# A feed-forward step with three of four k-tile groups by seven products, its down sums by ScalarE copy and accumulating DMA

## The chip, the cores and the metric

The kernel runs on one core of one Trainium2 chip. The metric is the time of one execution on the device in microseconds (us), as the median of three runs. Five engines of the core matter: TensorE (PE in the rows) multiplies, VectorE (DVE) and ScalarE (ACT) work elementwise on SBUF and PSUM, GpSimd (POOL) and SyncE (SP) issue DMAs here. Each works through its own list in order; semaphores tie the lists together.

## What is computed

One decoder layer for 256 tokens of width 2048 in float32: a feed-forward block, a mixing block with two attentions, a second feed-forward block, and a final norm. The change touches the two feed-forward blocks alone:

```python
def swiglu(x, w_gate, w_up, w_down):
    return (jax.nn.silu(x @ w_gate) * (x @ w_up)) @ w_down

x = x + 0.5 * swiglu(rmsnorm(x, ffn1_norm[l]), ffn1_w_gate[l], ffn1_w_up[l], ffn1_w_down[l])
...
x = x + 0.5 * swiglu(rmsnorm(x, ffn2_norm[l]), ffn2_w_gate[l], ffn2_w_up[l], ffn2_w_down[l])
```

The gate and up matrices are 2048 x 5632, the down matrix is 5632 x 2048.

## The kernel before

**Numbers in two parts.** Every float32 weight and activation is split into a rounded part (`hi`, made by ScalarE) and the rest (`lo`, made by VectorE), and each product of two matrices takes three matmuls: hi x hi, hi x lo, lo x hi.

**Slabs.** Weights arrive by DMA in pieces of 1 MB into `raw`, which has 4 places (`LOADS`). The unit of all three engines is a slab of 128 x 1024 weights. ScalarE rounds slab n into a ring of 6 places (`FFN_RING`; `w_hi` and `more_hi`) as soon as TensorE has finished slab n-6; VectorE then subtracts to get the `lo` half (`w_lo`, `more_lo`); TensorE multiplies. An ordinary slab is 12 matmuls of 512 columns (two k-tiles, two token tiles, three parts); a slab of kind "paired" holds one of the products below and is 6 matmuls.

**Chunks and steps.** The 5632 hidden columns are 11 chunks of 512. The first chunk's gate and up come in 16 slabs (`FIRST`). Then follow 10 steps (`STEPS`) of 30 slabs (`STEP`). Step i computes gate and up of chunk i+1 and multiplies chunk i's hidden values by the down matrix (the last 8 slabs, `DOWN`). The last chunk's down is in `last_down`. Nine steps are a loop with one step in its body; the tenth is written out.

**Seven products.** The 16 k-tiles are 4 groups of 4. For a group, two token tiles by (gate, up) is a 2 x 2 matrix product over pairs of k-tiles. In groups 1 and 3 ("paired") it is done by seven products (`PRODUCTS`) rather than eight, with sums of weights `T1` to `T4` (made by VectorE into `sums`) and sums of activations `S1` to `S4` (made once per block: `sum_pairs`, `split_pairs`). Groups 0 and 2 ("direct") are multiplied as they are, in 4 ordinary slabs. The seven results end in PSUM banks, and VectorE adds them up (lines 1397 to 1415 of the kernel before; semaphore `combined`).

**Around them.** When the products are added up, ScalarE applies silu and VectorE multiplies (`multiply_up`) into `hidden`. In the next step TensorE transposes it, the two token tiles one after the other through the same PSUM bank (`T`; `transpose_tokens`), ScalarE rounds (`round_tokens`) and VectorE splits each into `hT_hi` and `hT_lo` (`split_tokens`, line 1291). The second transpose waits until VectorE has read the first from the bank (`ht_lo`). Each of the four 512-column pieces of the down result is scaled by 0.5 and added to `xres` by VectorE from PSUM (`add_down`, line 1311).

The order is written out by hand: each engine's `step` goes over o = 0 to 29; ScalarE and VectorE at place o first handle slab o+6. SyncE loads a piece when `lo_ready` shows that the last user of its place is through (`FREE`).

Of the kernel before, what the change touches and what calls it, by code (L numbers as in the profile page):

```python
# [54 lines left out]
FIRST, STEP = 2 * WIDE, 30  # L55
# [19 lines left out]
PAIRED = {0: 0, 11: 1}  # L75
DIRECT = {7: 0, 18: 2}
T3, T1, T2, T4 = 0, 1, 2, 3
S1, S2, S3, S4 = 0, 1, 2, 3
PAIR_SLABS = 7

PRODUCTS = (("sum", T3), ("up", 1), ("sum", T1), ("sum", T2), ("sum", T4), ("gate", 1), ("gate", 0))
SUMS = 8 * STEPS

FREE = (-6, -4, -2, 0, 2, 7, 9, 11, 13, 18, 20, 22)
GROUP_ORDER = (1, 0, 3, 2)


def step_slab(r):

    for first, g in PAIRED.items():  # L90
        if first <= r < first + PAIR_SLABS:
            return "paired", g, r - first
    for first, g in DIRECT.items():
        if first <= r < first + 4:
            return "direct", g, r - first
    return "down", None, r - (STEP - DOWN)
# [27 lines left out]
class Place:  # L124
# [3 lines left out]
    def __init__(self, start, load, per=0, loads=0, i=None):  # L128
# [8 lines left out]
        assert per % self.ring == 0  # L137
# [5 lines left out]
    def slot(self, offset):  # L143
        return (self.start + offset - self.origin) % self.ring
# [15 lines left out]
def step_place(f, i=None):  # L160
    return Place(FFN_START[f] + FIRST, FFN_LOAD[f] + FIRST_LOADS, STEP, STEP_LOADS, i)


def final_step_place(f):
    return Place(FFN_START[f] + FIRST + (STEPS - 1) * STEP, FFN_LOAD[f] + FIRST_LOADS + (STEPS - 1) * STEP_LOADS)
# [6 lines left out]
def build(nc, x, ffn1_norm, ffn1_w_gate, ffn1_w_up, ffn1_w_down, mix_norm, w_in, b_forget,  # L172
# [39 lines left out]
    sums = nc.alloc_sbuf_tensor_at("sums", [P, 4, 2, CH], F32, offset=qT_at)  # L212
    pair_hi = nc.alloc_sbuf_tensor_at("pair_hi", [P, 4, 4, P], F32R, offset=kT_at)
    pair_lo = nc.alloc_sbuf_tensor_at("pair_lo", [P, 4, 4, P], F32R, offset=kT_at + 16 * P * 4)
# [72 lines left out]
    def step_source(r):  # L287

        kind, g, o = step_slab(r)
        if kind == "down":  # L290
            l = STEP_LOADS - NN + o // 2
            return raw[:, l % LOADS, o % 2 * 2:o % 2 * 2 + 2, :], l
        if kind == "direct":
            l = 2 * GROUP_ORDER.index(g) + o // 2
            return raw[:, l % LOADS, o % 2 * 2:o % 2 * 2 + 2, :], l
        what, which = PRODUCTS[o]
        if what == "sum":
            return sums[:, which], None
        l = 4 * g + (what == "gate")
        return raw[:, l % LOADS, which::2, :], l  # L300
# [23 lines left out]
    combined = sem("combined")  # L324
    hi_ready = sem("hi_ready")
# [55 lines left out]
    ADDED = {0: 2, "mix": 2 + FF_CHUNKS * NN, 1: 2 + (FF_CHUNKS + NN) * NN}  # L381
    ADDED_ALL = ADDED[1] + FF_CHUNKS * NN
# [13 lines left out]
    with block:  # L396

        @block.sync
        def _(sp):
# [27 lines left out]
            def ffn(f):  # L427
# [12 lines left out]
                with sp.Fori(0, STEPS) as i:  # L440
                    place = step_place(f, i)
                    cols = bass.ds(i * CH + CH, CH)
                    for l, g in enumerate(GROUP_ORDER):
                        order = (up_w, gate_w) if g % 2 else (gate_w, up_w)
                        for half, w in enumerate(order):
                            load_step(place, 2 * l + half, w[f][:, CT * g:CT * (g + 1), cols])
                    for n in range(NN):
                        load_step(place, 2 * NN + n, down_w[f][:, bass.ds(i * CT, CT), n * CH:(n + 1) * CH])
# [68 lines left out]
        def _(pe):  # L517
# [112 lines left out]
            def paired(place, offset, g):  # L630

                def of_pair(s):
                    return lambda j: (pair_hi[:, s, 2 * g + j], pair_lo[:, s, 2 * g + j])

                def of_tile(odd, t):
                    return lambda j: of_x(CT * (2 * g + 1) + 2 * j + odd, t)

                for o, (bank, lhs) in enumerate((
                        (M7, of_pair(S3)), (UP0, of_pair(S4)), (M5, of_pair(S1)), (M6, of_pair(S2)),
                        (GATE + 1, of_tile(1, 1)), (GATE, of_tile(1, 0)), (M1, of_tile(0, 0)))):  # L640
                    yield o
                    whole = bank in (M7, M5, M1, M6)
                    product(place, offset + o, bank, lhs, g == 0, whole and g == 1)

            def ffn(f, b):

                def step(place, i, last):
                    hid, base, merged = i * TT + HID[f], i * NN + ADDED[f], (i + f * STEPS) * COMBINED
                    for o in paired(place, 0, 0):
                        if o == 1:  # L650

                            pe.wait_ge(added, base - 1)
                        if o == 2:
                            transpose_tokens(hid, 0, T)
                        if o == 4:

                            pe.wait_ge(hidden_ready, hid + TT)
                            pe.wait_ge(added, base)

                    pe.wait_ge(ht_lo, hid + 1)  # L660
                    transpose_tokens(hid, 1, T)
                    for g, first in ((0, 7), (2, 18)):
                        if g == 2:
                            for o in paired(place, 11, 1):
                                pass
                        for o in range(2):
# [945 lines left out]
```

## Time and profile before

| | us |
|---|---|
| median of 3 runs (lowest, highest) | 2107.26 (2106.88, 2107.4) |
| the profiled execution: time, span of its rows | 2106.82, 2105.0 |
| TensorE busy | 2081.9 |
| VectorE busy | 1611.0 |
| ScalarE busy | 1095.1 |

The span runs from the first to the last recorded instruction; 1.8 us of the profiled execution lie around it. "Busy" counts instructions at work; a matmul's row is longer than its share of the engine, because matmuls overlap, so the distance between starts is what one costs.

### The profile page before, as it was taken

Reading aid. Unit: us, or ns where it says so; the run is one execution under the profiler, and the core shown is the slowest. Engines: PE = TensorE matmul, PEld = TensorE weight load, DVE = VectorE, ACT = ScalarE, POOL = GpSimd, SP = SyncE. Lnnn points to the kernel's source line nnn. Section 1 sums busy time; section 2 is a strip of 40 time slices with the busy share of each in tenths; the row PEclk is TensorE's granted clock in tenths of the full one; section 3 lists DMA queues with packets and bytes.
Section 4 is the critical chain, followed back from the end, with each engine's and each line's share of the span. In section 5 each row is a group of like instructions: output and inputs, shape, how many; then the busy total and the mean of one; then the engine's idle time right before and its main releaser. Section 6 shows DMA issues by size and latency. Waiting matters only on the chain.

```text
span 2105.0 us, 26528 instructions
## 1 busy us (share of the span) xinstructions
PE 2081.9 (99%) x9475; PEld 1727.4 (82%) x9475; DVE 1611.0 (77%) x1613; ACT 1095.1 (52%) x1259; POOL 2.6 (0%) x7
## 2 busy tenths in 40 slices
PE   8999999999999999999999999999999999999997
PEld 6888888888888888888888888888888888888886
DVE  7988988899888744444455655688998888998886
ACT  6555555554555444554554344465555555555553
POOL 0000000000000000000000000000000000000000
PEclk9999999999999999999999999999999999999999
DMA  7655556555565455545445655556565655465652
GB/s 270 220 189 189 199 199 212 204 177 204 190 209 200 140 182 196 181 160 170 159 154 197 200 198 192 188 185 215 170 212 185 219 203 203 163 219 179 219 204 96
DMA packets 202452, 402.88 MB, mean 191 GB/s; under 512 B 6417, under 2 KB 6593, under 8 KB 202273
## 3 DMA queue, kind: packets, MB, share of 16 engines
q1 hardware_dynamic: 202032, 401.64, 56.2%
q8 instruction: 34, 0.56, 0.1%
q0 software_dynamic: 160, 0.46, 0.1%
q14 instruction: 18, 0.14, 0.0%
q10 hardware_dynamic: 208, 0.08, 0.0%
HBM read 400.06 MB, written 2.10 MB: 191 GB/s over the span
## 4 chain that ended last, share of the span: by engine, by line
PE 95%; DVE 2%; ACT 1%; DMA 1%; issue 1%; SPq 0%; ACTq 0%; DVEq 0%
PE ps L530 21%; PE ps L532 21%; PE ps L531 21%; PE ps L545 6%; PE ps L543 6%; PE ps L544 6%; PE ps L707 3%; PE ps L709 3%; PE ps L708 3%; PE ps L595 1%; DMA raw<-in_ffn_w_gate 1%; DVE w_lo L1201 0%; PE ps L718 0%; PE ps L779 0%; ACT w_hi L922 0%
## 5 line engine op out<-in xcount | busy, mean ns | idle before, releaser
L1201 DVE TENSOR_TENSOR w_lo<-raw,w_hi 128x1024 fp32r<-128x1024 f32 x256 | 312.8, 1224 | 303.4 <-ACT w_hi L922 303.2
L922 ACT ACTIVATE w_hi<-raw 128x1024 fp32r<-128x1024 f32 x256 | 270.2, 1059 | 310.7 <-PE ps L532 310.5
L935 ACT ACTIVATE w_hi<-raw 128x1024 fp32r<-128x1024 f32 x280 | 297.0, 1061 | 221.9 <-PE ps L709 98.7
L1235 DVE TENSOR_TENSOR w_lo<-raw,w_hi 128x1024 fp32r<-128x1024 f32 x280 | 342.1, 1222 | 79.5 <-ACT w_hi L935 66.2
L530 PE MATMUL ps<-w_hi,xT_hi 128*128 128x512 f32 x816 | 321.3, 394 | 2.7 <-DVE w_lo L1201 2.7
L532 PE MATMUL ps<-w_hi,xT_lo 128*128 128x512 f32 x816 | 318.6, 390 | 0.0
L531 PE MATMUL ps<-w_lo,xT_hi 128*128 128x512 f32 x816 | 318.2, 390 | 0.0
L1235 DVE TENSOR_TENSOR more_lo<-raw,more_hi 128x1024 fp32r<-128x1024 f32 x160 | 195.6, 1223 | 43.5 <-ACT more_hi L935 34.1
L935 ACT ACTIVATE more_hi<-raw 128x1024 fp32r<-128x1024 f32 x160 | 169.6, 1061 | 110.7 <-PE ps L532 87.1
L530 PE MATMUL ps<-w_hi,hT_hi 128*128 128x512 f32 x576 | 224.4, 390 | 0.0
L532 PE MATMUL ps<-w_hi,hT_lo 128*128 128x512 f32 x576 | 224.1, 389 | 0.0
L531 PE MATMUL ps<-w_lo,hT_hi 128*128 128x512 f32 x576 | 224.1, 389 | 0.0
L935 ACT ACTIVATE w_hi<-sums 128x1024 fp32r<-128x1024 f32 x120 | 127.7, 1064 | 181.1 <-PE ps L532 94.4
L530 PEld LDWEIGHTS ps<-w_hi,xT_hi 128*128 128x128 f32 x816 | 153.7, 188 | 33.6 <-issue 3.1
L532 PEld LDWEIGHTS ps<-w_hi,xT_lo 128*128 128x128 f32 x816 | 153.5, 188 | 32.4
L531 PEld LDWEIGHTS ps<-w_lo,xT_hi 128*128 128x128 f32 x816 | 153.7, 188 | 30.8
L1235 DVE TENSOR_TENSOR w_lo<-sums,w_hi 128x1024 fp32r<-128x1024 f32 x120 | 146.5, 1221 | 7.7 <-ACT w_hi L935 4.6
L1311 DVE SCALAR_TENSOR_TENSOR xres<-ps,xres 128x1024 f32<-128x1024 f32 x104 | 126.8, 1219 | 14.1 <-PE ps L532 14.1
L532 PEld LDWEIGHTS ps<-w_hi,hT_lo 128*128 128x128 f32 x576 | 108.1, 188 | 22.5
L531 PEld LDWEIGHTS ps<-w_lo,hT_hi 128*128 128x128 f32 x576 | 108.1, 188 | 22.4
L530 PEld LDWEIGHTS ps<-w_hi,hT_hi 128*128 128x128 f32 x576 | 108.1, 188 | 22.3
L709 PE MATMUL ps<-w_hi,xT_lo 128*128 128x512 f32 x320 | 124.5, 389 | 0.0
(218 smaller groups left out, 3583.6 us busy)
## 6 DMA issues: line engine op xcount, KB each, us to landing
raw<-in_ffn_w_gate SPq DMA_DIRECT2D x88, 1024.0 KB, 5.0
raw<-in_ffn_w_up SPq DMA_DIRECT2D x88, 1024.0 KB, 5.0
raw<-in_ffn_w_down SPq DMA_DIRECT2D x88, 1024.0 KB, 5.1
raw<-in_w_in SPq DMA_DIRECT2D x80, 1024.0 KB, 5.0
raw<-in_w_out SPq DMA_DIRECT2D x16, 1024.0 KB, 5.0
raw<-in_w_proj_dil SPq DMA_DIRECT2D x8, 1024.0 KB, 5.1
raw<-in_w_proj_fox SPq DMA_DIRECT2D x8, 1024.0 KB, 5.0
xres<-in_x SPq DMA_DIRECT2D x4, 512.0 KB, 7.1
```

The source lines that it names most:

```text
L530: nc.tensor.matmul(acc, hi, hi_w[:, j], start=first and j == 0, stop=False)
L531: nc.tensor.matmul(acc, hi, lo_w[:, j], start=False, stop=False)
L532: done = nc.tensor.matmul(acc, lo, hi_w[:, j], start=False, stop=last and j == 1)
L543: nc.tensor.matmul(acc, hi, hi_w[:, j], start=first and j == 0, stop=False)
L544: nc.tensor.matmul(acc, hi, lo_w[:, j], start=False, stop=False)
L545: done = nc.tensor.matmul(acc, lo, hi_w[:, j], start=False, stop=last and j == 1)
L709: done = nc.tensor.matmul(acc, lo, hi_w[:, j], start=False, stop=last and j == 1)
L922: nc.scalar.activation(slot_hi(place, offset), raw_half(place, offset), ACT.Copy).then_inc(hi_ready, 1)
L935: nc.scalar.activation(slot_hi(place, offset), src, ACT.Copy).then_inc(hi_ready, 1)
L1201: nc.vector.tensor_tensor(slot_lo(place, offset), raw_half(place, offset), slot_hi(place, offset).bitcast(F32), ALU.subtract).then_inc(lo_ ...
L1235: nc.vector.tensor_tensor(slot_lo(place, offset), step_source(r)[0], slot_hi(place, offset).bitcast(F32), ALU.subtract).then_inc(lo_ready, 1)
L1311: nc.vector.scalar_tensor_tensor(xres[:, :, chunk(n)], ps[:, banks:banks + TT], factor, xres[:, :, chunk(n)], ALU.mult, ALU.add)\
```

## The change

- Groups 1, 2 and 3 go by seven products, group 0 is direct. A step has 33 slabs: products 0 to 6 and 7 to 13 (two groups in a row), 4 direct slabs (14 to 17), products 18 to 24, down slabs 25 to 32. The order within the seven is new.
- The four weight sums share two places of `sums` (`SUM_PLACE`): `T3` and `T2` one, `T1` and `T4` the other; `T4` is made one slab later than before.
- In all steps but the last of each block the down result goes another way: ScalarE copies each pair of banks, scaled by 0.5, into one of two halves of `gate_buf` (semaphore `down_copied`), and GpSimd issues a DMA that adds it to `xres` (`accum_op`; semaphores `down_added`). ScalarE's third and fourth copy first wait for the first and second DMA to land.
- The transposes of the hidden tiles stand before slabs 5 and 9 (before: 2 and 7), ScalarE's and VectorE's parts of them at places 6 and 10 (before: 2 and 5). The adding up moves to places 22 to 28.
- 33 is no multiple of the ring of 6, so a loop body of TensorE, ScalarE and VectorE holds two steps.

The core of the diff:

```diff
-FIRST, STEP = 2 * WIDE, 30
+FIRST, STEP = 2 * WIDE, 33
...
-PAIRED = {0: 0, 11: 1}
-DIRECT = {7: 0, 18: 2}
+PAIR_AT, PAIR_GROUPS, PAIR_SLABS = (0, 7, 18), (1, 2, 3), 7
+DIRECT_AT, DIRECT_GROUP = 14, 0
-PRODUCTS = (("sum", T3), ("up", 1), ("sum", T1), ("sum", T2), ("sum", T4), ("gate", 1), ("gate", 0))
+PRODUCTS = (("sum", T3), ("gate", 0), ("sum", T1), ("sum", T2), ("up", 1), ("sum", T4), ("gate", 1))
+SUM_PLACE = {T3: 0, T2: 0, T1: 1, T4: 1}
-FREE = (-6, -4, -2, 0, 2, 7, 9, 11, 13, 18, 20, 22)
+FREE = (-6, -4, -2, 0, 5, 7, 12, 14, 16, 18, 23, 25)
...   TensorE, step
-                    for o in paired(place, 0, 0):
+                    for o in paired(place, 0):
...
-                        if o == 2:
-                            transpose_tokens(hid, 0, T)
+                        if o == 5:
+                            transpose_tokens(hid, 0, T)
...
+                    for o in paired(place, 1):
+                        if o == 2:
+                            pe.wait_ge(ht_lo, hid + 1)
+                            transpose_tokens(hid, 1, T)
-                        pe.wait_ge(combined, merged + (1, 3, 5, 4)[n])
+                        pe.wait_ge(combined, merged + (1, 3, 4, 5)[n])
...   ScalarE, step
+                        if not last and o > DOWN_AT and (o - DOWN_AT) % 2 == 1:
+                            n = (o - DOWN_AT) // 2
+                            earlier = f * (STEPS - 1) + (n >= 2)
+                            act.wait_ge(slab_done, place.slab(o + 1))
+                            if not (type(i) is int and i + earlier == 0):
+                                act.wait_ge(down_added[(n + 2) % NN], i * 16 + earlier * 16)
+                            nc.scalar.activation(gate_buf[:, n % 2], ps[:, banks:banks + TT], ACT.Copy,
+                                                 scale=0.5).then_inc(down_copied, 1)
...   GpSimd
+            for j in range(2 * (STEPS - 1)):
+                for n in range(NN):
+                    pool.wait_ge(down_copied, j * NN + n + 3)
+                    if j > 0:
+                        pool.wait_ge(down_added[n], j * 16)
+                    pool.dma_start(xres[:, :, n * CH:(n + 1) * CH], gate_buf[:, n % 2],
+                                   accum_op=ALU.add).then_inc(down_added[n], 16)
...   VectorE, weight_sum and step
+                if kind == "paired" and o in (1, 2, 4):
+                    weight_sum(place, q, pair, {1: T1, 2: T2, 4: T4}[o], count)
+                if r + 1 in PAIR_AT:
+                    weight_sum(place, q, PAIR_AT.index(r + 1), T3, count)
-                        if o > STEP - DOWN and o % 2 == 1:
+                        if last and o > DOWN_AT and (o - DOWN_AT) % 2 == 1:
...
-                        if o == 2:
+                        if o == 6:
                             split_tokens(hid, 0, T)
-                        if o == 5:
+                        if o == 10:
                             split_tokens(hid, 1, T)
-                        if o == 18:
+                        if o == 22:
...
-                with dve.Fori(0, STEPS - 1) as i:
-                    step(step_place(f, i), i, False)
+                with dve.Fori(0, STEPS // 2 - 1) as i:
+                    for s in range(2):
+                        step(step_place(f, s, 2, i), i * 2 + s, False)
```

**VectorE at the start of a step.** The rows are those of the step written out last, where no loop's register rows stand between. `sums<-` rows are weight sums, `w_lo` and `more_lo` rows are splits of slabs, `hT_lo` rows the splits of the two token tiles. Before, from the split of slab 6 to that of the second token tile:

```order
L1235 TENSOR_TENSOR more_lo<-raw,more_hi 128x1024 [waits hi_ready] x2
L1235 TENSOR_TENSOR w_lo<-raw,w_hi 128x1024 [waits hi_ready]
L1291 TENSOR_TENSOR hT_lo<-ps,hT_hi 128x4x128 [waits ht_hi]
L1235 TENSOR_TENSOR w_lo<-raw,w_hi 128x1024 [waits hi_ready]
L1208 TENSOR_TENSOR sums<-raw 128x1024 [waits raw_landed0]
L1235 TENSOR_TENSOR w_lo<-raw,w_hi 128x1024 [waits hi_ready]
L1235 TENSOR_TENSOR w_lo<-sums,w_hi 128x1024 [waits hi_ready]
L1291 TENSOR_TENSOR hT_lo<-ps,hT_hi 128x4x128 [waits ht_hi]
```

Now, from the weight sum ahead of slab 6 (the first `hT_lo` row is the first token tile; slabs 6 to 12 stand before it):

```order
L1250 TENSOR_TENSOR sums<-raw 128x1024 [waits raw_landed2,lo_ready]
L1276 TENSOR_TENSOR w_lo<-raw,w_hi 128x1024 [waits hi_ready]
L1276 TENSOR_TENSOR w_lo<-sums,w_hi 128x1024 [waits hi_ready]
L1254 TENSOR_TENSOR sums<-raw 128x1024 [waits raw_landed3,lo_ready]
L1276 TENSOR_TENSOR w_lo<-raw,w_hi 128x1024 [waits hi_ready]
L1258 TENSOR_TENSOR sums<-sums,raw 128x1024 [waits summed,lo_ready]
L1276 TENSOR_TENSOR more_lo<-sums,more_hi 128x1024 [waits hi_ready] x2
L1262 TENSOR_TENSOR sums<-raw,sums 128x1024 [waits summed,lo_ready]
L1276 TENSOR_TENSOR w_lo<-raw,w_hi 128x1024 [waits hi_ready]
L1276 TENSOR_TENSOR w_lo<-sums,w_hi 128x1024 [waits hi_ready]
L1332 TENSOR_TENSOR hT_lo<-ps,hT_hi 128x4x128 [waits ht_hi]
```

Before, three splits (slabs 6 to 8) stood ahead of the first token tile; now there are seven (slabs 6 to 12) and four weight sums.

**TensorE at the second transpose.** Again the last written-out step. Before, the last three matmuls of slab 6, the second transpose, which waits for `ht_lo`, and the start of slab 7, a direct one:

```order
L543 MATMUL ps<-more_hi,xT_hi 128x512
L544 MATMUL ps<-more_lo,xT_hi 128x512
L545 MATMUL ps<-more_hi,xT_lo 128x512
L595 MATMUL ps<-tab,hidden 128x128 [waits hidden_ready,ht_lo]
L595 MATMUL ps<-tab,hidden 128x128 x3
L530 MATMUL ps<-more_hi,xT_hi 128x512 [waits lo_ready]
L531 MATMUL ps<-more_lo,xT_hi 128x512
L532 MATMUL ps<-more_hi,xT_lo 128x512
```

Now, the last three of slab 8, the transpose, and the start of slab 9, a product:

```order
L552 MATMUL ps<-w_hi,xT_hi 128x512
L553 MATMUL ps<-w_lo,xT_hi 128x512
L554 MATMUL ps<-w_hi,xT_lo 128x512
L604 MATMUL ps<-tab,hidden 128x128 [waits hidden_ready,ht_lo]
L604 MATMUL ps<-tab,hidden 128x128 x3
L552 MATMUL ps<-w_hi,pair_hi 128x512 [waits lo_ready]
L553 MATMUL ps<-w_lo,pair_hi 128x512
L554 MATMUL ps<-w_hi,pair_lo 128x512
```

The second transpose stands nine products into the step, where it stood seven in; between the two transposes there are four products (slabs 5 to 8), where there were five (slabs 2 to 6).

**ScalarE in the down part.** Before, only roundings of slabs and the two rows of silu stood there. Now, from the first copy to the fourth, in the ninth step of a block (`gate_buf` rows are the copies, the other `raw` and `sums` rows the roundings):

```order
L1074 ACTIVATE gate_buf<-ps 128x1024 [waits down_added2,slab_done]
L950 ACTIVATE w_hi<-sums 128x1024 [waits slab_done,summed]
L998 ACTIVATE chunk_buf<-chunk_buf,rstd 128x512 [waits rstd_ready,combined]
L998 ACTIVATE chunk_buf<-chunk_buf,rstd 128x512
L950 ACTIVATE w_hi<-raw 128x1024 [waits slab_done,raw_landed1]
L1074 ACTIVATE gate_buf<-ps 128x1024 [waits down_added3,slab_done]
L950 ACTIVATE w_hi<-sums 128x1024 [waits slab_done,summed]
L950 ACTIVATE more_hi<-sums 128x1024 [waits slab_done,summed]
L1074 ACTIVATE gate_buf<-ps 128x1024 [waits down_added0,slab_done]
L950 ACTIVATE more_hi<-raw 128x1024 [waits slab_done,raw_landed0]
L950 ACTIVATE w_hi<-sums 128x1024 [waits slab_done,summed]
L1074 ACTIVATE gate_buf<-ps 128x1024 [waits down_added1,slab_done]
```

The four copies are new; roundings of slabs stand between them, and each waits for the DMA that last read its half of `gate_buf`.

## Rows read from the trace of the kernel before

**Rows 1.** The page, busy us (share of the span) xinstructions, and the chain's shares

```profile
PE 2081.9 (99%) x9475; PEld 1727.4 (82%) x9475; DVE 1611.0 (77%) x1613; ACT 1095.1 (52%) x1259; POOL 2.6 (0%) x7
...
PE 95%; DVE 2%; ACT 1%; DMA 1%; issue 1%; SPq 0%; ACTq 0%; DVEq 0%
```

**Rows 2.** Waits of TensorE: engine line waited for, us, times, longest

```profile
PE ps L576 <- DMA xres<-in_x: 6.1, 1, 6.1
PE ps L530 <- DVE w_lo L1201: 2.7, 1, 2.7
```

**Rows 3.** Line 1400 (once a step), 300 to 420 us: durations ns, first and last start

```profile
L1400 DVE TENSOR_TENSOR partial<-ps,partial x2: 691/691/691, 351.3 to 414.8; 128x512 f32<-128x512 f32 x2
```

**Rows 4.** Window of one step: stretch, length, busy of TensorE, its loads, VectorE, ScalarE

```profile
314.60:378.10 63.50, 63.50 (x286) 52.56 (x285) 56.65 (x51) 34.32 (x35) 0.00 (x0) 1.00 0.57 198
```

**Rows 5.** Timeline of TensorE, end of a step and start of the next

```profile
303.67 0.39 PE L530 MATMUL ps<-w_hi,hT_hi 128*128 128x512 f32 x1
...
313.87 0.39 PE L530 MATMUL ps<-w_hi,hT_hi 128*128 128x512 f32 x1
...
314.55 0.39 PE L543 MATMUL ps<-more_hi,pair_hi 128*128 128x512 f32 x1
...
317.27 0.60 PE L595 MATMUL ps<-tab,hidden 128*128 128x128 f32 x4
317.63 0.48 PE L543 MATMUL ps<-w_hi,pair_hi 128*128 128x512 f32 x1
...
320.46 0.39 PE L543 MATMUL ps<-w_hi,xT_hi 128*128 128x512 f32 x1
```

**Rows 6.** Timeline of VectorE around the same place and later in the step

```profile
301.35 1.41 DVE L1305 SCALAR_TENSOR_TENSOR hidden<-up_sums,rstd,chunk_buf 128x512 f32<-128x512 f32 x2
...
305.01 1.22 DVE L1224 TENSOR_TENSOR sums<-raw 128x1024 f32<-128x1024 f32 x1
...
311.81 2.54 DVE L1235 TENSOR_TENSOR w_lo<-sums,w_hi 128x1024 fp32r<-128x1024 f32 x2
...
315.89 1.22 DVE L1235 TENSOR_TENSOR w_lo<-raw,w_hi 128x1024 fp32r<-128x1024 f32 x1
...
321.54 0.68 DVE L1291 TENSOR_TENSOR hT_lo<-ps,hT_hi 128x512 fp32r<-128x512 f32 x1
...
349.45 1.23 DVE L1235 TENSOR_TENSOR more_lo<-raw,more_hi 128x1024 fp32r<-128x1024 f32 x1 [1.49 <-ACT more_hi L935]
350.59 0.68 DVE L1397 TENSOR_TENSOR partial<-ps,partial 128x512 f32<-128x512 f32 x1
```

**Rows 7.** Timeline of ScalarE, the same step

```profile
314.75 1.06 ACT L935 ACTIVATE w_hi<-raw 128x1024 fp32r<-128x1024 f32 x1 [1.66 <-PE ps L532]
...
346.60 0.58 ACT L1049 ACTIVATE partial<-ps 128x512 f32<-128x512 f32 x1
```

**Rows 8.** DMA issues of the whole run: KB each, median us to landing

```profile
tab<-shape_tables POOLq DMA_DIRECT2D x1, 384.0 KB, 6.3
...
f_raw<-in_w_in POOLq DMA_DIRECT2D x1, 64.0 KB, 7.4
```

**Rows 9.** Windows at launch: stretch, length, PE busy, granted clock, DMA share, GB/s

```profile
10.00:14.00 4.00, 1.30 (x5) 0.93 1.05 387
14.00:16.00 2.00, 2.00 (x7) 0.50 1.05 387
16.00:18.00 2.00, 2.00 (x9) 0.79 1.06 388
```

**Rows 10.** Timeline of TensorE at launch

```profile
13.81 0.63 PE L530 MATMUL ps<-w_hi,xT_hi 128*128 128x512 f32 x1
...
16.80 0.42 PE L531 MATMUL ps<-w_lo,xT_hi 128*128 128x512 f32 x1
```

**Rows 11.** Timelines at launch, of GpSimd and then of VectorE

```profile
16.03 0.68 POOL L1185 DMA_DIRECT2D tab<-shape_tables  x1 [15.58 <-ACT xT_hi L947]
...
16.70 2.36 DVE L1201 TENSOR_TENSOR w_lo<-raw,w_hi 128x1024 fp32r<-128x1024 f32 x2 [0.25 <-ACT w_hi L922]
```

More of the change, by code:

```diff
@@ L287, in step_source @@
     def step_source(r):
[L289 to L300, printed above, removed]
+        kind, pair, o = step_slab(r)
+        if kind == "paired":
+            what, which = PRODUCTS[o]
+            if what == "sum":
+                return sums[:, SUM_PLACE[which]], None
+            l = PAIR_LOADS[pair][what == "gate"]
+            return raw[:, l % LOADS, which::2, :], l
+        l = DIRECT_LOADS[o // 2] if kind == "direct" else DOWN_LOADS + o // 2
+        return raw[:, l % LOADS, o % 2 * 2:o % 2 * 2 + 2, :], l
     ident = tab[:, C_ID:C_ID + P]
@@ L324, in build @@
     combined = sem("combined")
+    down_copied = sem("down_copied")
+    down_added = [sem(f"down_added{n}") for n in range(NN)]
     hi_ready = sem("hi_ready")
@@ L674, in step @@
+                    for o in range(2):
+                        slab(place, DIRECT_AT + o, (GATE, GATE + 1), of_x, CT * DIRECT_GROUP + 2 * o,
+                             False, False)
+                    pe.wait_ge(ht_lo, hid + TT)
+                    for o in range(2):
+                        direct_up(place, DIRECT_AT + 2 + o, CT * DIRECT_GROUP + 2 * o, o == 0, o == 1)
+                    for o in paired(place, 2):
+                        pass
                     for n in range(NN):
-                        pe.wait_ge(combined, merged + (1, 3, 5, 4)[n])
+                        pe.wait_ge(combined, merged + (1, 3, 4, 5)[n])
@@ L706, in direct_up @@
                         begin = first and j == 0 and t == 1
+                        end = last and j == 1 and t == 1
                         nc.tensor.matmul(acc, hi, hi_w[:, j], start=begin, stop=False)
                         nc.tensor.matmul(acc, hi, lo_w[:, j], start=False, stop=False)
-                        done = nc.tensor.matmul(acc, lo, hi_w[:, j], start=False, stop=last and j == 1)
+                        done = nc.tensor.matmul(acc, lo, hi_w[:, j], start=False, stop=end)
                 done.then_inc(slab_done, 1)
@@ new lines, in step @@
+                        if last and o == DOWN_AT + 4:
+                            for n in (2, 3):
+                                act.wait_ge(down_added[n], (f + 1) * (STEPS - 1) * 16)
+                            round_hidden(i * TT + HID[f] + TT, last_hi, A)
+                for s in range(2):
+                    step(step_place(f, s), s, False)
+                with act.Fori(1, STEPS // 2 - 1) as i:
+                    for s in range(2):
+                        step(step_place(f, s, 2, i), i * 2 + s, False)
@@ L1234, in split_step @@
+                kind, pair, o = step_slab(r)
+                if kind == "paired" and o in (1, 2, 4):
+                    weight_sum(place, q, pair, {1: T1, 2: T2, 4: T4}[o], count)
+                if r + 1 in PAIR_AT:
+                    weight_sum(place, q, PAIR_AT.index(r + 1), T3, count)
+                if r == STEP - 1 and not final:
+                    weight_sum(place, q + 1, 0, T3, count)
                 dve.wait_ge(hi_ready, place.slab(offset + 1))
```

256 lines of the change are left out of this document (126 added, 130 removed).

## Prediction

> **What bounds the kernel now.** I read the page first: TensorE is busy for 2081.9 of 2105.0 us, and the chain that ended last runs through it for 95% [rows 1]. Its list of waits says how close to its limit it is: after the first microseconds of launch (6.1 and 2.7 us) nothing over 1.0 us is in it [rows 2]. So a matmul less is time gained, and a new wait of TensorE is time lost; everything else counts only through these two.
>
> The sizes come from the timelines. Matmuls start 0.2267 us apart: from 303.67 to 313.87 us there are 45 steps, 10.20 / 45 [rows 5]. A product slab (6 matmuls) is 1.36 us, an ordinary one (12) 2.72. A transpose of one token tile takes 317.27 to 317.63, and the two products behind it 2.83 (to 320.46) instead of 2.72, so it costs 0.36 + 0.11 = 0.47 [rows 5]. A step of before is 276 matmuls and two transposes, 62.57 + 0.94 = 63.51 us; line 1400, which runs once a step, comes back after 414.8 - 351.3 = 63.5 [rows 3]. The sum closes, so no wait hides in a step, and TensorE is busy throughout [rows 4].
>
> VectorE's operations of 1024 columns start 1.133 us apart when it has work: six of them lie between 305.01 and 311.81 [rows 6]. Their results are ready 1.22 after the start.
>
> **The change, part by part.**
>
> *Matmuls.* 30 slabs with 14 products were 14 x 6 + 16 x 12 = 276 matmuls; 33 slabs with 21 products are 21 x 6 + 12 x 12 = 270. Six fewer are 1.36 us a step, 27.2 us in 20 steps. This part is nearly certain.
>
> *VectorE's load.* A step gains 3 splits and 4 weight sums and loses 4 additions of the down result: 3 x 1.133 = 3.4 us more, in steps that are to be shorter. In a step of before it was busy for 56.65 of 63.50 us [rows 4], so the sum over a step still fits. What counts is where the work stands.
>
> *The stretch of 14 products.* I take time 0 at the first product of a step; in the trace it is 314.55 [rows 5]. ScalarE can round slab 5 once the last down slab is through: it started 0.20 after time 0 (314.75) and took 1.06 [rows 7], so with 0.04 for the hand-over VectorE starts on slab 5 at 1.30. (In the trace it did so at 315.89, 1.34, with an addition ahead of it [rows 6].) This holds it at the start of every step, however early it was before. Up to the split of the first token tile its list now has 12 operations: slabs 5 to 12 and the sums T3, T1, T2, T4 of the second group. 12 x 1.133 = 13.60. Three times a sum and the split of its slab have one other operation between them, while sum, hand-over, rounding and hand-over take 1.22 + 0.04 + 1.06 + 0.04 = 2.36 against 2 x 1.133; that adds 0.09 each, 0.27. The token split starts at 15.17 and takes 0.68 [rows 6]; at 15.9 TensorE may go on. TensorE reaches the second transpose after nine products and one transpose, 9 x 1.36 + 0.47 = 12.71. It waits **3.2 us, in every step**. Before, the same split was done at 321.54 + 0.68, which is 7.67 after time 0, and wanted at 7 x 1.36 + 0.47 = 9.99: it had 2.3 us to spare. What is queued behind the waiting transpose is all of TensorE's work. After it VectorE has slack again (four direct slabs of 2.72 us), so nothing is late next. Bounds: without the 0.27 and with the quickest hand-overs 2.9; with 2% on VectorE's operations 3.5.
>
> *The start of the down part.* Its first bank pair waits for the first addition behind slab 28's split, which needs slab 22 done. From the end of slab 22: 0.20, rounding 1.06, 0.04, then split to addition 1.14 (349.45 to 350.59), addition 0.68 [rows 6, 7], 0.05: 3.17. TensorE has two products for it, 2.72. A wait of 0.45, between 0.3 and 0.6. Before, it had two direct slabs and more.
>
> *The tenth step.* Here the hidden tiles are wanted within the step, after the fourth down slab. That is at 21 x 1.36 + 8 x 2.72 + 0.94 + 3.2 + 0.45 = 54.9. VectorE starts the first partial addition at 54.9 - 10.88 - 0.05 - 0.68 = 43.3; it and the second take 1.3 together, then seven operations at 1.133 (slabs 29 to 32, two additions of the up result, one of the down result) lead to the adding up of the gate, at 52.5; then slab 33; a down addition that must wait for slab 28 (54.9 and 0.2, so 55.1); slab 34 at 56.2; the multiplication at 57.4. Its first half is ready 0.7 later (1.41 for both [rows 6]). TensorE waits 3.3, and 0.2 for the second tile: 3.5 us, twice in the program, 7.0. Bounds 5 and 9.
>
> *Down sums.* ScalarE takes on four copies a step. 512 columns from PSUM took 0.58 [rows 7], so 1024 take at most 1.16; ScalarE is busy for half the span [rows 1]. At the start of a step the fourth copy makes slab 6's rounding late by 0.7 us, but VectorE comes to slab 6 later still (3.57, behind T3). The third copy waits for the DMA issued after the first. From copy to copy there are four down slabs, 10.9 us; less the copy of 1.1, the transfer has 9.8 us from GpSimd's start. The trace has no accumulating DMA. The nearest rows are GpSimd's two: 6.3 us for 384 KB, and 7.4 for 64 KB in 2048 short pieces [rows 8], both beside full queues (share 1.05 in [rows 9]). Scaled by bytes, 6.3 x 512 / 384 = 8.4, an estimate that leaves 1.4. I cost it at nothing; the lower bound is nothing too, the upper one is 12 us, if reading the destination adds as much as half the transfer: 2.2 us late, in 18 steps, 40 us. GpSimd's issue did not slow VectorE at launch: two splits beside it took 2.36, which is 1.133 + 1.22 [rows 11].
>
> *Two turns per body.* Before, any gap at the end of the body is within the 0.01 us by which the step closed: nothing.
>
> *The clock.* A wait of TensorE may cost more than its length. At launch it waited 2.7 us [rows 2]; the granted clock then was 0.93, 0.50 (the lower level, 1.2 GHz) and 0.79 in the next windows [rows 9], and seven matmuls from 13.81 to 16.80 started 0.427 apart instead of 0.227 [rows 10], 1.4 us lost, with the edges 1.6. The new waits are longer, and there are 22 of them: 35 us if each does it. But ahead of that wait stood a few transposes, ahead of these a full stretch of matmuls, which speaks for less. Between 0 and 35 I take half, 17. The Trainium skill, TensorE: Matmul & The Clock Gate, "HAM oscillation — how this bites in real kernels", says that a kernel whose TensorE waits for operands once in each tile can fall to the lower clock in every one of them. By that rule the upper bound would be the value, and the time 2195; the launch rows agree as far as they go.
>
> **The sum**, against the profiled execution's own 2106.8 (0.4 under the median): 2106.8 - 27.2 + 20 x 3.65 + 7.0 + 17 = 2176.6, say **2177 us**, 3.3% slower. Without the clock it is 2160, with all of it 2195.
>
> **The rivals.** Beside the forecast:
> 1. *Every long wait brings the lower clock*, the upper bound above: 2195. For it speak the launch rows [rows 9, 10], against it the full matmuls ahead of each wait. Chance 0.20. The same page of the Trainium skill gives this outcome.
> 2. *The work saved comes through.* If the token split is early enough at nine products, only 27.2 us are left: 2080, faster by 1.3%. It turns on one place: VectorE would have to reach the token tile 3.2 us, three operations, earlier; from a wait under 0.9 us on, the change is a gain. For it: VectorE's slack over a step. Against it: slab 5 is tied to the end of the step before, and 12 operations at 1.133 are plain. Chance 0.06.
> 3. *The accumulating DMA becomes the bound*, above 9.8 us. Each microsecond more makes the third copy, the roundings behind it and so the step late by about one: at 12 us 2177 + 40 = 2217, at 15 us over 2260. For it: nothing in the trace adds by DMA, and four transfers a step share the engines with 12 MB of weights. Against it: the rows above. Chance 0.10.
> 4. *Gain and wait cancel.* The wait would have to be 0.9 us. Chance 0.02.
>
> **How the numbers follow.** The forecast has 0.62; its own range is 2151 (no loss of clock, the 20 waits 0.3 and 0.15 shorter) to 2190. With rival 1 and its upper bounds (waits 0.3 and 0.15 longer, 2204) the range is 2148 to 2208, which leaves out rivals 2 to 4, 0.18. A measurement of this kernel tells about 0.2% from no change (the runs spread by 0.03%). Faster 0.06, same 0.02, slower 0.92.
>
> **What would show it.** TensorE's waits should name the token split of VectorE (`hT_lo`) behind the second transpose, some 3.2 us in each step, 64 in all; and the first partial addition with 9. The step should be near 65.8 us plus the clock. The granted clock should stand under 1.00 in windows just behind those waits if they cost what I put on them, and at 1.00 if not. `down_added` should not appear among ScalarE's waits, and landings should be 6 to 9 us. I am wrong if the token split's wait is under 1 us, or if ScalarE's copies wait for DMAs.

## The result, and the profile after

| | before | after |
|---|---|---|
| time, median of 4 runs | 2107.14 us (2106.88 to 2107.4) | 2205.82 us (2205.49 to 2206.17) |
| ratio, 95% interval | | 1.0468 (1.0455 to 1.0481) |
| profiled execution, span | 2105.0 us | 2203.9 us (its time 2206.02) |

The changed kernel is 4.7% slower, 99 us. The page of the changed kernel, its busy times and the chain that ended last, and two rows on the accumulating DMAs (the queue with its packets, MB and share; the issue with KB and median us to landing):

```profile
PE 2096.4 (95%) x9355; PEld 1723.3 (78%) x9355; DVE 1690.2 (77%) x1691; ACT 1215.0 (55%) x1393; POOL 87.6 (4%) x80
...
q0 software_dynamic: 19744, 38.22, 9.9%
...
PE 76%; DVE 11%; issue 7%; ACT 5%; DMA 1%; DVEq 0%; SPq 0%; ACTq 0%
...
xres<-gate_buf POOLq DMA_DIRECT2D x72, 512.0 KB, 6.1
```

Against [rows 1], TensorE has 120 matmuls fewer, 20 x 6, and still more busy time, and the chain that ended last now runs through VectorE for 11%. Part of this is a lower clock: the mean granted clock of the run is 0.982, where it was 0.997, and the windows below show where it fell. TensorE's list of waits says where the rest is (engine line waited for, us, times, longest):

```profile
PE ps L604 <- DVE hT_lo L1332: 68.4, 20, 5.9
PE ps L539 <- DVE partial L1437: 7.7, 20, 0.6
PE ps L604 <- DVE hidden L1346: 6.5, 2, 3.3
PE ps L585 <- DMA xres<-in_x: 6.1, 1, 6.1
PE ps L539 <- DVE w_lo L1237: 2.7, 1, 2.7
PE ps L552 <- DVE w_lo L1276: 1.5, 3, 0.6
```

The fourth and fifth row are those of before [rows 2]; the first three are new, and are the three places that the prediction named: the split of the first token tile ahead of the second transpose, the first partial addition at the start of the down part, and `hidden` in the tenth step. The first of them, in the timelines of one step, first TensorE's first product, then VectorE:

```profile
336.67 0.39 PE L552 MATMUL ps<-more_hi,pair_hi 128*128 128x512 f32 x1
...
337.96 1.23 DVE L1276 TENSOR_TENSOR w_lo<-sums,w_hi 128x1024 fp32r<-128x1024 f32 x1 [1.49 <-ACT w_hi L950]
339.11 1.22 DVE L1250 TENSOR_TENSOR sums<-raw 128x1024 f32<-128x1024 f32 x1
...
348.51 1.22 DVE L1262 TENSOR_TENSOR sums<-raw,sums 128x1024 f32<-128x1024 f32 x1
349.65 1.22 DVE L1276 TENSOR_TENSOR w_lo<-raw,w_hi 128x1024 fp32r<-128x1024 f32 x1
350.93 1.23 DVE L1276 TENSOR_TENSOR more_lo<-sums,more_hi 128x1024 fp32r<-128x1024 f32 x1
352.07 0.68 DVE L1332 TENSOR_TENSOR hT_lo<-ps,hT_hi 128x512 fp32r<-128x512 f32 x1
```

Slab 5's split starts 1.29 after the first product, twelve operations (that split is the first) follow one another, and the first token tile's split starts at 15.40, counted from the first product. TensorE, which had run its last matmul ahead of the transpose at 349.18, goes on at 352.81, and then does not run at its old pace. Its timeline, and its windows behind this wait and behind the wait of a later step (stretch, length, busy, granted clock, DMA share, GB/s):

```profile
349.18 0.39 PE L554 MATMUL ps<-w_hi,xT_lo 128*128 128x512 f32 x1
352.81 0.66 PE L604 MATMUL ps<-tab,hidden 128*128 128x128 f32 x4 [3.25 <-DVE hT_lo L1332]
...
353.91 0.63 PE L554 MATMUL ps<-w_hi,pair_lo 128*128 128x512 f32 x1
354.34 0.63 PE L552 MATMUL ps<-w_hi,pair_hi 128*128 128x512 f32 x1
...
356.90 0.44 PE L552 MATMUL ps<-w_hi,pair_hi 128*128 128x512 f32 x1
357.18 0.39 PE L553 MATMUL ps<-w_lo,pair_hi 128*128 128x512 f32 x1
```

```profile
352.00:354.00 2.00, 1.19 (x7) 0.89 0.90 265
354.00:356.00 2.00, 2.00 (x6) 0.50 1.05 357
356.00:358.00 2.00, 2.00 (x8) 0.75 1.01 391
...
488.00:490.00 2.00, 1.43 (x9) 1.00 0.95 296
490.00:492.00 2.00, 2.00 (x10) 1.00 0.95 346
```

From 353.91 on seven matmuls start 0.427 us apart instead of 0.227, at the lower of the two clock levels (0.50, 1.2 GHz). At 488.57 a wait of the same 3.25 us leaves the clock at 1.00. I call it a fall when the granted clock goes to 0.50 at such a wait, and a period the time from one step's line 1440 to the next one's, since that line runs once a step. What a fall costs can be read from it (durations in ns, first and last start in us), here over a step without and one with a fall:

```profile
L1440 DVE TENSOR_TENSOR partial<-ps,partial x2: 690/690/691, 450.4 to 516.7; 128x512 f32<-128x512 f32 x2
```

```profile
L1440 DVE TENSOR_TENSOR partial<-ps,partial x2: 691/691/691, 314.7 to 382.6; 128x512 f32<-128x512 f32 x2
```

66.3 and 67.9 us, against 63.5 before [rows 3]: a fall costs 1.6 us. Of the 18 periods between neighbouring steps of a block, 14 have one. Four long waits lie outside the periods, in both blocks that for the token tile in the first step (5.9 and 5.0 us) and that for `hidden` in the tenth (3.3 us), and all four have one.

### The profile page after: what moved, and what is told of

Read it like the earlier page. It is cut to its first block, busy times and chain, and to the rows that moved or that the text cites. A ratio compares the mean times of both kernels' runs of the same rounds, so it can differ in the third digit from the quotient of the medians.

```text
span 2203.9 us, 26783 instructions
## 1 busy us (share of the span) xinstructions
PE 2096.4 (95%) x9355; PEld 1723.3 (78%) x9355; DVE 1690.2 (77%) x1691; ACT 1215.0 (55%) x1393; POOL 87.6 (4%) x80
## 4 chain that ended last, share of the span: by engine, by line
PE 76%; DVE 11%; issue 7%; ACT 5%; DMA 1%; DVEq 0%; SPq 0%; ACTq 0%
PE ps L539 18%; PE ps L541 18%; PE ps L540 18%; PE ps L553 4%; PE ps L552 4%; PE ps L554 4%; DVE w_lo L1276 3%; ACT w_hi L950 2%; PE ps L723 2%; PE ps L722 2%; PE ps L724 2%; ACT more_hi L950 1%; DVE sums L1262 1%; DVE sums L1250 1%; PE ps L604 1%
## 5 line engine op out<-in xcount | busy, mean ns | idle before, releaser
L539 PE MATMUL ps<-w_hi,xT_hi 128*128 128x512 f32 x856 | 336.8, 393 | 2.7 <-DVE w_lo L1237 2.7
L541 PE MATMUL ps<-w_hi,xT_lo 128*128 128x512 f32 x856 | 334.0, 390 | 0.0
L950 ACT ACTIVATE w_hi<-sums 128x1024 fp32r<-128x1024 f32 x160 | 169.9, 1062 | 214.3 <-PE ps L541 65.2
L1276 DVE TENSOR_TENSOR w_lo<-sums,w_hi 128x1024 fp32r<-128x1024 f32 x160 | 195.6, 1223 | 63.5 <-ACT w_hi L950 61.4
L1276 DVE TENSOR_TENSOR more_lo<-raw,more_hi 128x1024 fp32r<-128x1024 f32 x140 | 171.0, 1222 | 36.1 <-ACT more_hi L950 32.5
L950 ACT ACTIVATE more_hi<-raw 128x1024 fp32r<-128x1024 f32 x140 | 148.0, 1057 | 88.0 <-PE ps L554 43.4
L539 PEld LDWEIGHTS ps<-w_hi,xT_hi 128*128 128x128 f32 x856 | 161.2, 188 | 35.3 <-issue 3.0
L1222 POOL DMA_DIRECT2D xres<-gate_buf x72 | 84.9, 1179 | 1997.2 <-ACT gate_buf L1074 1946.5
L950 ACT ACTIVATE more_hi<-sums 128x1024 fp32r<-128x1024 f32 x80 | 84.9, 1062 | 107.0 <-DVE sums L1250 24.8
L552 PE MATMUL ps<-w_hi,pair_hi 128*128 128x512 f32 x300 | 123.1, 410 | 0.6 <-DVE w_lo L1276 0.6
L553 PE MATMUL ps<-w_lo,pair_hi 128*128 128x512 f32 x300 | 122.0, 407 | 0.0
```

What stands on the lines that cost most here:

```text
L539: nc.tensor.matmul(acc, hi, hi_w[:, j], start=first and j == 0, stop=False)
L541: done = nc.tensor.matmul(acc, lo, hi_w[:, j], start=False, stop=last and j == 1)
L552: nc.tensor.matmul(acc, hi, hi_w[:, j], start=first and j == 0, stop=False)
L553: nc.tensor.matmul(acc, hi, lo_w[:, j], start=False, stop=False)
L950: nc.scalar.activation(slot_hi(place, offset), src, ACT.Copy).then_inc(hi_ready, 1)
L1222: pool.dma_start(xres[:, :, n * CH:(n + 1) * CH], gate_buf[:, n % 2], accum_op=ALU.add).then_inc(down_added[n], 16)
```

## The experiments

Nine kernels were run, in three groups, each beside runs of the kernel before (2106.8 to 2107.2 us) on the same chip. Times are medians, ratios are to the kernel before. The wait that all but the fourth speak of is that of TensorE ahead of the second transpose, in which it waits for VectorE's split of the first token tile.

**The transpose three slabs later (e1).** Otherwise the changed kernel; VectorE's work and the DMAs are all there.

```diff
@@ TensorE, step(): for o in paired(place, 1)
-                        if o == 2:
+                        if o == 5:
                             pe.wait_ge(ht_lo, hid + 1)
                             transpose_tokens(hid, 1, T)
@@ ScalarE and VectorE, step(): rounding and splitting of the second tile
-                        if o == 10:
+                        if o == 11:
```

> The changed kernel with one thing moved: the transpose of the second token tile, and VectorE's fetch of its result, three resp. one place later (ahead of slab 12 instead of slab 9), so that TensorE reaches it about 0.7 us after VectorE has written hT_lo instead of 3.25 us before. Nothing is taken out of VectorE's work, no DMA is changed. Theory of the token wait (with the clock that falls behind it): of the changed kernel's 2206 us, 20 waits with the pipeline's emptying (71.6 us) go except in the two tenth steps (some 3.3 us each stay), and with them most of the some 31 us of slow matmuls: 2106.8 - 27.2 + 10.9 (the wait for the first partial addition) + 6.8 (tenth steps) + some 3 = 2100 us, 2095 to 2112, a period of one step near 62.6 us and a granted clock back above 0.99. Rival that VectorE's added work or the accumulating DMAs bound the step: the wait only turns up at another place, the time stays above 2170 us. Rival that the clock's fall is a thing of its own and not of the waits: about 2130 us, with slow matmuls still in most steps.

Measured: 2109.51 us (2109.05 to 2110.73), ratio 1.0014 (1.0004 to 1.0024): 96.3 us less than the changed kernel, from another place for one transpose (four matmuls) and one place later for the rounding and the split that follow it. The list of waits and line 1440 over one step:

```profile
PE ps L539 <- DVE partial L1437: 7.7, 20, 0.6
PE ps L604 <- DVE hidden L1346: 6.6, 2, 3.3
...
PE ps L552 <- DVE w_lo L1276: 2.3, 5, 0.6
...
PE ps L604 <- DVE hT_lo L1332: 0.2, 1, 0.2
```

```profile
L1440 DVE TENSOR_TENSOR partial<-ps,partial x2: 692/692/692, 357.4 to 420.2; 128x512 f32<-128x512 f32 x2
```

The token wait went from 68.4 to 0.2 us, no period has a fall, and the other two waits are unchanged. Both rivals fall: no wait above 0.6 us turned up at another place, and the clock fell only behind the two waits of 3.3 us that are left in the tenth steps. The 2109.5 lies at the upper end of what I expected. The mean granted clock is 0.997, as before the change.

**The transpose one slab later (e2).** The first of the two edits above with `o == 3`, nothing else.

> The changed kernel with the transpose of the second token tile one place later (ahead of slab 10 instead of slab 9), so that the wait for VectorE's token split in each step is shorter by one slab's matmuls, some 1.9 us instead of 3.25. It asks what the clock makes of a shorter wait. If a wait of 1.9 us brings no slow matmuls: 20 x (1.9 + 0.16 + 0.53) + 6.8 on 2106.8 - 27.2, which is 2138 us, a period near 64.5 us. If it brings them as the wait of 3.25 us does, in some 18 of 22 cases at 1.7 us each: 2169 us. Rival that the step is bound by something else than this wait: no less than 2195 us.

Measured: 2158.03 us (2155.5 to 2158.49), ratio 1.0239 (1.0222 to 1.0256). The wait was 1.9 us in an ordinary step, and one of 18 periods had a fall (66.5 against 64.9 us). It lies between my two numbers, 20 above the one without falls: a step took 64.9 and not 64.5 us, the first step of each block waited 3.6 and 3.7 us, and the four long waits of the first and tenth steps all had a fall. Against e1's 62.8 us a wait of 1.89 us by its row costs 2.1: rows of waits run from the modelled end of the last matmul (0.39 after its start), while the next could have started after 0.23. That is 0.16 of the 0.2.

**All three waits moved (e3).** e1, and four edits more: the partial additions one slab earlier, and so the activation and the multiplication that make hidden.

```diff
@@ VectorE, step()
-                        if o == 22:
+                        if o == 21:
                             dve.wait_ge(slab_done, place.slab(22))
...
-                        if o == 26:
+                        if o == 25:
                             dve.wait_ge(slab_done, place.slab(DOWN_AT))
...
-                        if o == 28:
+                        if o == 27:
                             dve.wait_ge(combined, merged + 4)
@@ ScalarE, step()
-                        if o == 27:
+                        if o == 26:
                             act.wait_ge(combined, merged + 5)
```

> The kernel of the run with the transpose ahead of slab 12, with two more things moved by one place: VectorE's partial additions of the products of the group before come one slab earlier (so that the 0.39 us wait at the start of the down part goes) and the activation and the multiplication that make hidden one slab earlier. Theory: the 10.9 us of the partial addition's wait go too, and part of the tenth steps' wait: 2106.8 - 27.2 + some 4 = 2084 us, 2078 to 2095, and a period of one step near 62.1 us, 1.4 us (six matmuls of 0.227 us) below the kernel before. If instead VectorE's work or the DMAs bound the step, the time doesn't fall below that of the other kernel by more than 3 us.

Measured: 2088.72 us (2088.63 to 2088.9), ratio 0.9914 (0.9897 to 0.993), the fastest of all: faster than before by 18.1 us. The window of one step (stretch, length, busy of TensorE, its loads, VectorE, ScalarE and GpSimd, granted clock, DMA share, GB/s), the waits that are left beside those at launch and between the blocks, and line 1222, GpSimd's accumulating DMA:

```profile
353.30:415.46 62.16, 62.16 (x280) 51.47 (x279) 59.23 (x55) 39.99 (x43) 4.71 (x4) 1.00 0.79 236
```

```profile
PE ps L552 <- DVE w_lo L1276: 2.9, 6, 0.6
PE ps L604 <- DVE hidden L1346: 2.4, 2, 1.2
...
PE ps L552 <- DVE more_lo L1276: 0.6, 1, 0.6
PE ps L604 <- DVE hT_lo L1332: 0.3, 2, 0.2
```

```profile
DMA to landing us min/median/max: 5.3/7.8/8.4
```

TensorE is busy throughout the step again, as in [rows 4], and the step is 62.16 us: 63.51 less six matmuls of 0.2267, 62.15. So the saved matmuls are real and worth the 27.2 us that were put on them. What is missing to 2106.8 - 27.2 = 2079.6 is 9 us, and stands in the four rows: eleven waits, all in the first and the tenth step of a block, 6.2 us by their rows, and each costs 0.2 to 0.3 more than its row says.

**Two turns alone (e5).** The kernel before, with two steps in one loop body.

```diff
-                with pe_loop(STEPS - 1) as i:
-                    step(step_place(f, i), i, False)
+                with pe_loop(STEPS // 2 - 1) as i:
+                    for s in range(2):
+                        step(turn_place(f, s, 2, i), i * 2 + s, False)
+                step(turn_place(f, STEPS - 2), STEPS - 2, False)
```

(and so on ScalarE and VectorE)

> The kernel before with only the loop bodies changed: two steps of the down loop in one body, as in the changed kernel, and nothing else. My prediction gave this nothing: 2107 us, within 2 us. Rival that longer bodies cost instruction loading or gain from fewer branches: over 4 us away, to be seen as idle time at a body's start.

Measured: 2107.59 us (2107.24 to 2108.12), ratio 1.0004 (0.9994 to 1.0013). No new wait at a body's start. This part is nothing, as costed.

**The down additions back on VectorE (e4, e6).** e4 is e3, e6 the changed kernel in its own order, both without the ScalarE copies and without the accumulating DMAs.

```diff
@@ ScalarE, step()
-                            nc.scalar.activation(gate_buf[:, n % 2], ps[:, banks:banks + TT], ACT.Copy,
-                                                 scale=0.5).then_inc(down_copied, 1)
@@ GpSimd
-                    pool.dma_start(xres[:, :, n * CH:(n + 1) * CH], gate_buf[:, n % 2],
-                                   accum_op=ALU.add).then_inc(down_added[n], 16)
@@ VectorE, step()
-                        if last and o > DOWN_AT and (o - DOWN_AT) % 2 == 1:
+                        if o > DOWN_AT and (o - DOWN_AT) % 2 == 1:
                             n = (o - DOWN_AT) // 2
-                            dve.wait_ge(down_added[n], (f + 1) * (STEPS - 1) * 16)
                             add_down(place, o + 1, n, DOWN_BANKS[n], 0.5)
```

> The kernel of the run with all three waits moved (2088.7 us), with the down additions back on VectorE: no copies on ScalarE, no accumulating DMAs. It shows what the accumulating DMAs buy. VectorE gets four operations of 1.133 us a step, 4.5 us, and would be busy for about 61.5 of 62.2 us. Theory that VectorE has no room left for them: TensorE gets waits of some 1.3 us a step in pieces under 1 us, no slow matmuls, so 2088.7 + 20 x 1.3 = 2115 us, 2105 to 2130. Rival that the slack takes them all: 2089. Rival that the accumulating DMAs and the issuing GpSimd hold VectorE up: below 2089.

> The changed kernel (2205.8 us) in its own order, with only the down additions back on VectorE. Two of these additions then stand in the stretch of 14 products, ahead of the split of the second token tile: one beside the end of the step before, so that slab 5's split starts later, one within. If the token wait is what VectorE's list says, it grows by one to one and a half operations, from 3.25 to 4.4 to 5 us, and each is followed by slow matmuls: 2206 + 20 x 1.2 to 1.6 = 2230 to 2238 us, and a period of some 69.3 us. Rival that the accumulating DMAs cost about what they save: 2206.

Measured: e4 2115.9 us (2115.81 to 2115.97), ratio 1.0043 (1.0026 to 1.0059), 27.2 more than e3; e6 2241.1 us (2240.54 to 2242.23), ratio 1.0639 (1.0621 to 1.0657), 35.3 more than the changed kernel. A step's window and the first wait in e4's list, and the first in e6's:

```profile
359.90:423.80 63.90, 62.98 (x280) 51.24 (x278) 63.35 (x59) 36.01 (x39) 0.00 (x0) 1.00 0.56 198
```

```profile
PE ps L552 <- DVE w_lo L1254: 11.3, 23, 0.6
```

```profile
PE ps L604 <- DVE hT_lo L1310: 92.6, 20, 5.9
```

In e4 VectorE is busy for 63.35 of 63.90 us and TensorE waits for it in small pieces: VectorE is the bound, and the time ends above that of the kernel before. So the products without the DMAs lose 0.4% even in the better order; with them they gain 0.9%. In e6 the token wait is 4.6 us in an ordinary step, all 22 long waits are followed by slow matmuls, and the time is 3 us above my range.

**The length of a wait and the clock (e7, e8, e9).** e2 with idle operations of VectorE that add two pieces of a table into a buffer that is free at that time. e7 has one at place 10, ahead of the second tile's split; e8 one and e9 two (the second into `chunk_buf[:, 1]`) at place 6, ahead of the first tile's:

```diff
                         if o == 6:
+                            nc.vector.tensor_tensor(chunk_buf[:, 0], tab[:, 0:CH], tab[:, P:CH + P], ALU.add)
                             split_tokens(hid, 0, T)
```

> For the clock alone: the kernel with the transpose ahead of slab 10 (a wait of 1.9 us in each step, slow matmuls after one of 18), with one idle operation of VectorE (two 512-column pieces of the table added into a buffer that is free then, 0.69 us) ahead of the second token split. The wait should be 2.6 us in each step, and without any loss of clock the time 2158 + 20 x 0.69 = 2172 us. If the length of the wait decides whether the clock falls, some steps (between 1 and 14 of 18) lose 1.7 us each: 2175 to 2195. If it is a matter of where in the step the wait stands (one slab later than in the changed kernel), it stays at 2172 with one or two falls.

> The operation of the run before stood behind the split that TensorE waits for: its wait ahead of slab 10 is for the split of the first token tile, and the idle operation filled time in which VectorE had nothing to do. Here the same operation (512 columns, 0.69 us) stands ahead of the first tile's split, in the kernel with the transpose ahead of slab 10. The wait should be 1.9 + 0.6 to 0.7 = 2.5 to 2.6 us in each step; without loss of clock the time is 2157 + 20 x 0.65 = 2170 us. If the clock falls for waits above a length, 1 to 14 of 18 steps lose 1.7 us each and the time is 2172 to 2194; if it depends on where in the step the wait stands, 2170.

> As the run with one idle operation, with two (each 512 columns, 0.69 us): a wait of some 3.2 us in each step, as long as in the changed kernel, but one slab later. Without loss of clock 2157 + 20 x 1.3 = 2183 us. If the length of the wait is what counts, 14 to 18 steps lose 1.7 us, as in the changed kernel, and the time is 2207 to 2214; if the place counts, it stays near 2183.

Measured: e7 2156.34 us (2156.01 to 2157.57), ratio 1.0234 (1.0217 to 1.0251); e8 2177.52 us (2175.65 to 2180.28), ratio 1.0339 (1.032 to 1.0357); e9 2201.26 us (2196.72 to 2203.15), ratio 1.0442 (1.0424 to 1.0461). e7 missed its purpose by a misreading of mine: the wait is for the first tile's split, and an operation behind it changed nothing; both of its expected numbers, 2172 and 2175 to 2195, were wrong. It is of use as a second look at 1.89 us. e8 lies in the range that I put on length, e9 6 us below it and 18 above the number for place. Line 1441 of e8 over two steps in turn, the first with a fall and the second without, and its windows behind the waits of these two steps:

```profile
L1441 DVE TENSOR_TENSOR partial<-ps,partial x2: 691/691/691, 375.4 to 442.5; 128x512 f32<-128x512 f32 x2
```

```profile
L1441 DVE TENSOR_TENSOR partial<-ps,partial x2: 690/690/691, 442.5 to 508.1; 128x512 f32<-128x512 f32 x2
```

```profile
414.00:416.00 2.00, 1.88 (x9) 0.79 0.95 370
416.00:418.00 2.00, 2.00 (x7) 0.50 0.79 199
481.00:483.00 2.00, 1.73 (x10) 1.00 0.96 367
483.00:485.00 2.00, 2.00 (x11) 1.00 0.85 228
```

67.1 and 65.6 us. Counted over the 18 periods of each profiled execution:

| kernel | wait in an ordinary step, us | periods with a fall, of 18 |
|---|---|---|
| e1 | 0.37 (start of the down part) | 0 |
| e7 / e2 | 1.89 | 0 / 1 |
| e8 | 2.49 | 6 |
| e9 | 3.10 | 13 |
| changed kernel | 3.25 | 14 |
| e6 | 4.6 | 18 |

The share of falls goes with the length, and not with the place: e2, e8 and e9 wait at the same place, and e9, one slab later than the changed kernel, loses the clock almost as often. At 1.9 us the clock was kept in 35 of 36 periods, at 4.6 it fell each time, and between them the share of falls rises. The waits outside the periods fit: over all traces each of the 30 waits of 3.6 us and more had a fall. The same wait in the same kernel may go either way; in e8 the falls come two or three steps apart. The launch wait of 2.7 to 2.9 us, the same in every kernel here, had a fall in four of the eleven profiled executions: in that of the kernel before, e2, e3 and e5, and not in that of the changed kernel, whose windows from 10 to 18 us all stand at 1.00.

The counts are those of one execution each, and they differ from run to run. The runs of e8 and e9 spread by 0.2 and 0.3%, those of e3 and of the kernel before by 0.01 to 0.04%, and the mean granted clock of each run goes with its time: in e9 0.985 at 2196.7 us and 0.982 at 2203.2, in e8 0.990 at 2175.7 and 0.987 at 2180.3. At 1.6 us a fall, the spreads of 6.4 and 4.6 us are some four and three falls. In e1 four of ten runs took 2110.5 to 2110.7 us at 0.995 and the other six 2109.1 to 2109.6 at 0.996 to 0.997, about one fall between them.

## Why the prediction was right, and which term was mis-sized

The direction, the place and the mechanism held. The size did not: the time, 2205.8, is 29 us above the forecast's 2177 and above 2151 to 2190, the forecast's own part of the range. It is inside the whole range only because that was drawn up to 2208 for rival 1 with its upper bounds (2204), and what came is rival 1, which had a chance of 0.20. Of the 29 us, 13 are the clock, 7 the first step of each block, 4 each the token wait and the start of the down part. These terms all went the same way, so no error hid another, and that the total still fell inside the range is partly luck.

- *Matmuls, -27.2.* Right. e3's step is 62.16 us, and 120 records fewer are on the page.
- *The stretch of 14 products, 3.2 us a step.* Right. Slab 5's split at 1.29 (I had 1.30), the token split at 15.40 (15.17): the three gaps between a sum and the split of its slab are 0.15 each and not 0.09, and the operations start 1.138 apart. TensorE went on at 16.14 instead of 15.9, after being due at 12.74 (349.18 + 0.23, less 336.67), so it lost 3.4 us where the row says 3.25. e1 shows the cause: with the transpose moved and all of VectorE's work and the DMAs kept, 96.3 us came back.
- *The start of the down part, 0.45.* The row says 0.37, its price is more: from e1 to e3 the period falls from 62.83 to 62.16, 0.67 us. 13 us in 20 steps, where I had 9.
- *The tenth step, 3.5 us.* 6.5 in two waits by their row. Right.
- *The first step of each block.* A miss. I took it for a step like the others. There the token wait was 5.9 and 5.0 us, and in the first block four slabs ahead of it were late by 0.4 to 0.6 us each (line 1276 in the list). By the rows that is 4.5 us more in token waits and 2.1 in slabs: 6.6 us that I had at nothing.
- *Down sums, nothing.* Right at this pace. Landings took 5.3 to 9.7 us, 6.1 in the median, under the 9.8 us that I had worked out; my estimate of 8.4 was too high. `down_added` holds ScalarE up once, for 0.2 us. In e3, where the loads are denser, the median landing is 7.8 us and ScalarE's copies wait 17 times, 0.7 us at most, though TensorE never does: rival 3 has no place here, but its margin is small. What I had not asked is what the copies and DMAs buy: 35 us here and 27 in e3.
- *Two turns, nothing.* Right, e5.
- *The clock, 17 us between 0 and 35.* This is the term that was mis-sized. I halved it because a full stretch of matmuls stands ahead of each wait, unlike at launch. That argument carried nothing: 18 of 22 waits were followed by slow matmuls, 14 x 1.6 in the periods, and 2.6, 1.8, 1.6 and 1.4 us for the other four (the 60 matmuls behind each, against the same 60 where no fall came), together 30 us. The launch wait of 2.7 us [rows 2, 9, 10], the only long wait for VectorE in the trace of before, gave the right price of a fall, 1.6 us. That it had a fall in that trace was not certain: the same wait in the changed kernel had none. So it could not tell how many of the new waits would have one. The rule that I had quoted from the Trainium skill (TensorE: Matmul & The Clock Gate, "HAM oscillation — how this bites in real kernels") gave the upper bound; the runs agree with it for most waits of 3 us and for all of 3.6 us and more. Waits of 1.9 us once in each step, shorter than those of its example (3 to 5 us), left the clock up in 35 of 36 periods.

The sum with measured terms, against the profiled execution's 2206.0: 2106.8 - 27.2 + 68 (20 x 3.4) + 13 + 7 + 6.6 + 30 = 2204. The 2 us left are not accounted for.

Rival 2, that the work saved comes through, fell by where one transpose stands: in e1 and e3 the same work is there, and e3 is faster than before by what the rival promised less 9 us. Rival 4, gain and wait cancel, needed a token wait of 0.9 us, and it was 3.25. e1 comes out where this rival stood, by other waits: those that are left to it take back the 27.2 us and 2.7 more.

What stays open: why a wait of 2.5 to 3.3 us is followed by a fall in one step and not in the next, and whether e3's eleven waits could be moved away as well. No kernel was run for either.

## What to carry to other kernels

Less work on the engine that bounds the kernel shortens the cover of everything behind it: for each hand-over back to that engine, work out at what time it is now due and when the other engine's list reaches it. Three slabs' difference in the place of one transpose decided between 4.7% and 0.1% slower, and with the partial additions and the making of `hidden` one slab earlier too the kernel was 0.9% faster. Share of busy time did not show it: VectorE stood at 77% before and after. Count the loss of clock behind the matmul engine's long waits as well: here it came in 6 of 18 periods at 2.5 us, and in the changed kernel it added 30 us to waits of some 95.

## What the hardware showed that I had not expected

- Whether the clock falls behind a wait is a matter of degree: it did none or one time of 18 at 1.9 us, 6 at 2.5, 13 at 3.1, 14 at 3.25, all at 4.6, and each time at the 30 waits of 3.6 us and more; in an ordinary step a fall cost 1.6 us (seven matmuls 0.427 apart instead of 0.227).
- An accumulating DMA between two buffers in SBUF, 512 KB, landed in 6.1 us (5.3 to 9.7) beside loads, and in 7.8 when these were denser. GpSimd's issue took 1.18 us, and VectorE's operations of 1024 columns started 1.13 us apart beside it, as without it (changed kernel, medians).
- A wait's row understates its price by 0.2 to 0.3 us: 0.37 cost 0.67, 1.89 cost 2.1. Of this 0.16 is that the row starts at the modelled end of the last matmul; the rest is not explained.
